# One group of transposes in place of three: own rows, sample rows and sample residual

## The reference

```python
q = (xf @ w_q).reshape(n, PEER_HEADS, 2, PEER_DK // 2)
s = jnp.einsum('nhpd,hpkd->nhpk', q, sub_keys)
sv, si = lax.top_k(s, PEER_TOPK)                # 16 of 128 keys, twice
...                                             # 16 of the 256 pairs: eidx (experts), g (gates)
act = gelu(jnp.einsum('nd,ned->ne', xt, u[it])) * gt
y = jnp.einsum('ne,ned->nd', act, v[it])
h = h + y
```

## Time and profile before

| | |
|---|---|
| median of the runs, us | 1998.24 (1996.53 to 1999.02) |
| the profiled execution, us | 1998.43 |
| its span in the trace, us | 1996.6 |
| share of busy time | PE 98%, DVE 77%, ACT 43%, POOL 35% |
| granted clock of TensorE | 0.997 of full speed |
| DMA, mean over the span | 266 GB/s |

### The profile page before, as it was taken

One profiled execution on the slowest core, in us unless ns is written; L12 is line 12 of the kernel. 1 busy time (PEld: TensorE's weight loads), 2 busy tenths in 40 slices (PEclk: granted clock), 3 DMA queues, 4 the chain that ended last, 5 costly groups with the idle time before them and its releaser, 6 DMA issues.

```text
span 1996.6 us, 29304 instructions
## 1 busy us (share of the span) xinstructions
PE 1960.7 (98%) x11128; PEld 1748.1 (88%) x11128; DVE 1532.0 (77%) x2295; ACT 856.1 (43%) x865; POOL 701.6 (35%) x496
## 2 busy tenths in 40 slices
PE   7999999999999999999999999999999999999998
PEld 6997777998999999999999999988888888888886
DVE  4998756556788899889888997567777767778776
ACT  4340135434535555545455545533343433334343
POOL 2010101220526687888876883010100101113410
PEclk9999999999999999999999999999999999999999
DMA  5463295443444788888888898899988899998984
GB/s 209 162 202 132 98 383 207 148 168 127 152 145 149 258 275 273 291 279 293 279 291 280 313 338 288 295 343 345 344 325 332 328 349 352 361 354 342 376 316 145
DMA packets 101227, 531.29 MB, mean 266 GB/s; under 512 B 19376, under 2 KB 21568, under 8 KB 45792
## 3 DMA queue, kind: packets, MB, share of 16 engines
q1 hardware_dynamic: 71552, 408.93, 57.1%
q0 software_dynamic: 24304, 106.45, 14.4%
q10 hardware_dynamic: 5296, 14.98, 2.0%
HBM read 491.34 MB, written 38.14 MB: 265 GB/s over the span
## 4 chain that ended last, share of the span: by engine, by line
PE 88%; DVE 6%; issue 2%; ACT 2%; DMA 1%; POOL 0%; DVEq 0%; SPq 0%; ACTq 0%; POOLq 0%
PE acc L1616 18%; PE mis L1994 17%; PE acc L1994 17%; PE acc L1617 9%; PE acc L1593 5%; PE acc L1595 5%; PE acc L1594 5%; PE acc L1642 5%; PE acc L1736 2%; DVE wl L932 2%; DMA raw<-in_u 1%; PE mis L1711 1%; ACT wh L545 1%; DVE xhl L940 0%; PE mis L1687 0%
## 5 line engine op out<-in xcount | busy, mean ns | idle before, releaser
L932 DVE TENSOR_TENSOR wl<-raw,wh 128x2048 fp32r<-128x2048 f32 x310 | 711.3, 2296 | 280.0 <-ACT wh L545 263.8
L545 ACT ACTIVATE wh<-raw 128x2048 fp32r<-128x2048 f32 x310 | 593.2, 1915 | 568.4 <-DMA raw<-in_v 403.7
L1616 PE MATMUL acc<-xhl,wh 128*128 128x448 f32 x2048 | 643.1, 374 | 1.0 <-DVE wl L932 1.0
L1617 PE MATMUL acc<-xhl,wl 128*128 128x224 f32 x2048 | 541.2, 264 | 0.0
L1616 PEld LDWEIGHTS acc<-xhl,wh 128*128 128x128 f32 x2048 | 384.1, 188 | 31.5 <-DVE wl L932 2.0
L1617 PEld LDWEIGHTS acc<-xhl,wl 128*128 128x128 f32 x2048 | 390.7, 191 | 0.0
L2152 POOL DMA_INDIRECT G<-gsum,cell x224 | 342.7, 1530 | 79.8 <-issue 68.2
L1593 PE MATMUL acc<-xhl,wh 128*128 128x288 f32 x736 | 220.7, 300 | 15.0 <-DVE wl L968 14.1
L1594 PE MATMUL acc<-xhl,wh 128*128 128x288 f32 x736 | 217.7, 296 | 0.0
L1595 PE MATMUL acc<-xhl,wl 128*128 128x288 f32 x736 | 217.4, 295 | 0.0
L2108 POOL DMA_INDIRECT ring<-in_ur,eidx x32 | 38.6, 1206 | 334.5 <-DVE hs L1421 325.9
(11 more groups left out here) (336 smaller groups left out, 2633.1 us busy)
## 6 DMA issues: line engine op xcount, KB each, us to landing
raw<-in_u SPq DMA_DIRECT2D x128, 1024.0 KB
raw<-in_v SPq DMA_DIRECT2D x128, 1024.0 KB
raw<-in_w_mix SPq DMA_DIRECT2D x28, 1024.0 KB
G<-zero SPq DMA_DIRECT2D x16, 1024.0 KB, 13.6
raw<-in_w_out SPq DMA_DIRECT2D x16, 1024.0 KB
raw<-in_w_pq SPq DMA_DIRECT2D x16, 1024.0 KB
gin<-G SPq DMA_DIRECT2D x32, 512.0 KB
h<-hbg ACTq DMA_DIRECT2D x32, 448.0 KB
```

What stands on the lines that cost most here:

```text
L545: act.activation(wh[:, n % 4], raw[:, n % 4], ACT.Copy).then_inc(hi_done, 1)
L932: dve.tensor_tensor(wl[:, n % 4], raw[:, n % 4], wh[:, n % 4].bitcast(F32), ALU.subtract).then_inc(lo_done, 1)
L1616: pe.matmul(acc[:, s, 0:2 * NU], wh[:, s, j, :], xu[:, j, 0:2 * NU], start=(j == 0), stop=False)
L1617: ins = pe.matmul(acc[:, s, 0:NU], wl[:, s, j, :], xuh[:, j, :], start=False, stop=(j == DT - 1))
```

## The change

The three groups become one, in step 2 of u. `xs4` is now filled with four different things: own columns (part 0 and 3), the sample's normed columns (part 1, by DVE, `sample_rows` moved from step 114 to step 0) and the sample's residual columns (part 2). One `turn_rows` makes rows of all three. ACT copies them out in steps 3 and 4, two banks each. In step 5 it writes partitions 32 to 63 to DRAM (`sample_rows`) and 64 to 95 (`hst_rows`), and in step 6, when both have landed, it copies the own rows from partitions 0 to 31 over these two parts, inside SBUF. The first own dot waits for that. In SP's program the sample rows are loaded back into the four parts of `xrow`, 256 KB each, one after each of the tiles 124 to 127. The first load has a wait for the last own dot ahead of it, behind a wait for the own tokens' hidden values that was there before. The sample's dots, Gelu and sums all stand two steps of v later. PE's groups 29 and 30 are back in the loop.

```diff
-V_DOTS = {2 * n: n for n in range(PICKS)}
-V_GELU = 2 * PICKS
+V_DOTS = {2 * n + 2: n for n in range(PICKS)}
+V_GELU = 2 * PICKS + 2
...
                     load_own_hidden(0)
+                    sp.wait_ge(dot_a_done, PICKS_A)
+                    sp.wait_ge(xr_out, 16)
+                if 124 <= n < 124 + P // NS:
+                    q = n - 124
+                    sp.dma_start(xrow[NS * q:NS * q + NS, :], dr["xr"]).then_inc(xrow_in, 16)
...
+            def row_copies():
+
+                act.wait_ge(xrow_out, 4)
+                act.dma_start(dr["xr"], xrow_a[NS:2 * NS, :]).then_inc(xr_out, 16)
+                act.dma_start(dr["hst"], xrow_a[2 * NS:3 * NS, :]).then_inc(hst_out, 16)
+
+            def row_repeats():
+
+                act.wait_ge(xr_out, 16)
+                act.wait_ge(hst_out, 16)
+                for q in (1, 2):
+                    act.dma_start(xrow_a[NS * q:NS * q + NS, :], xrow_a[0:NS, :]).then_inc(xrow_a_in, 16)
+
+            def rows_together():
+
+                act.wait_ge(xs_ready, 1)
+                for q in (0, 3):
+                    act.activation(xs4[:, :, q, :], xs[:], ACT.Copy).then_inc(xs4_ready, 1)
+                act.activation(xs4[:, :, 2, :], hT[:, :, NP_:N], ACT.Copy).then_inc(xs4_ready, 1)
...
-                if n == 4 * XROW_IT - 1:
-                    four_times(2)
-                if 3 <= n < 7:
-                    row_evac(xrow_a, n - 3, 1)
...
+                for c in ROW_EVACS.get(n, ()):
+                    row_evac(c)
+                if n == ROW_COPIES:
+                    row_copies()
+                if n == ROW_REPEATS:
+                    row_repeats()
...
-            with pe.Fori(1, XROW_IT) as i:
+            with pe.Fori(1, 31) as i:
                 for s in range(4):
                     u_slot(i, s)
             for s in range(4):
-                u_slot(XROW_IT, s)
-                if s == TURN_S:
-                    pe.wait_ge(xrow_out, 4)
-                    pe.wait_ge(xs4_ready, 2)
-                    turn_rows()
-            for s in range(4):
-                u_slot(HST_IT, s)
-                if s == TURN_S:
-                    pe.wait_ge(xrow_out, 8)
-                    for c in range(DT):
-                        ins = pe.transpose(mis[0:NS, c // 4, P * (c % 4):P * (c % 4) + P], hT[:, c, NP_:N], ident)
-                    ins.then_inc(hst_turned, 1)
-            for s in range(4):
                 u_slot(31, s)
```

More of the change, by code:

```diff
@@ L74 @@
 RSTD = (1, 0, 0, 1, 0)
-XROW_IT, HST_IT, TURN_S = 29, 30, 1
-XROW_EVAC, HST_EVAC = 4 * XROW_IT + TURN_S + 1, 4 * HST_IT + TURN_S + 1
+ROW_EVACS, ROW_COPIES, ROW_REPEATS = {3: (0, 1), 4: (2, 3)}, 5, 6
 CO_NEXT = {8: 2, 11: 3}
@@ L309, in build @@
                 xs4 = sb(o, "xs4", [P, DT, P // NS, NS])
-            with ExitStack() as o:
-                hst = sb(o, "hst", [P, D])
         ring_a = (ring_a0, ring_a1, ring_a2)
@@ L373, in build @@
         dot_done, sgelu_done, sact_ready, vsum_done = sem("dot_done"), sem("sgelu_done"), sem("sact_ready"), sem("vsum_done")
-        hst_turned, hst_copied, hst_out, hst_in = sem("hst_turned"), sem("hst_copied"), sem("hst_out"), sem("hst_in")
+        xrow_in, xrow_a_in, hst_out, hst_in = sem("xrow_in"), sem("xrow_a_in"), sem("hst_out"), sem("hst_in")
+        xr_out = sem("xr_out")
         res_turned, part_in, part_sum = sem("res_turned"), sem("part_in"), sem("part_sum")
@@ L824, in _, with row_evac @@
             act.sem_inc(gelu_done, 1)
-            def row_evac(to, c, count):
+            def row_evac(c):
                 if c == 0:
[L829 to L840, removed]
+                    act.wait_ge(xrow_turned, 1)
+                act.activation(xrow_a[:, 512 * c:512 * c + 512], mis[:, c, :], ACT.Copy).then_inc(xrow_out, 1)
+            def row_copies():
[12 more added lines that the diff above has]
+                act.activation(xs4[:, :, 2, :], hT[:, :, NP_:N], ACT.Copy).then_inc(xs4_ready, 1)
             def gelu_a(c):
@@ L858, in u_hook @@
                 if n == 1:
-                    four_times(1)
-                if n == 4 * XROW_IT - 1:
-                    four_times(2)
-                if 3 <= n < 7:
-                    row_evac(xrow_a, n - 3, 1)
[L864 to L871, removed]
+                    rows_together()
+                for c in ROW_EVACS.get(n, ()):
[4 more added lines that the diff above has]
+                    row_repeats()
                 if n == 4 * 31 + 2:
@@ L1401, in sample_rows @@
             def sample_rows():
-                dve.wait_ge(xrow_turned, 1)
-                own.done(dve.tensor_tensor(xs[:], hT[:, :, NP_:N], bcast(par[:, Q_GFFN:Q_GFFN + DT], NS, 2), ALU.mult))
+                dve.wait_ge(xs_ready, 1)
+                at = xs4[:, :, 1, :]
+                own.done(dve.tensor_tensor(at, hT[:, :, NP_:N], bcast(par[:, Q_GFFN:Q_GFFN + DT], NS, 2), ALU.mult))
                 own.wait(0)
-                dve.tensor_tensor(xs[:], xs[:], bcast(rstd[:, 1, NP_:N], DT, 1), ALU.mult).then_inc(xs_ready, 1)
+                dve.tensor_tensor(at, at, bcast(rstd[:, 1, NP_:N], DT, 1), ALU.mult).then_inc(xs4_ready, 1)
             def own_dot(g):
@@ L1411, in own_dot @@
                     dve.wait_ge(xrow_out, 4)
+                    dve.wait_ge(xrow_a_in, 32)
                 dve.wait_ge(pick_a_in[own_ring(g)], 16 * len(ring_users(g)))
@@ L1418, in pick_dot @@
                 if g == 0:
-                    dve.wait_ge(xrow_out, 8)
+                    dve.wait_ge(xrow_in, 16 * (P // NS))
                 dve.wait_ge(pick_in[g % 2], 16 * (g // 2 + 1))
@@ L1461, in u_extras @@
                     own_x()
+                    sample_rows()
                 if n == 4:
@@ L1938, in _ @@
                     pe.wait_ge(pq_out, 16)
-                    pe.wait_ge(xs4_ready, 1)
+                    pe.wait_ge(xs4_ready, 4)
                     turn_rows()
-            with pe.Fori(1, XROW_IT) as i:
+            with pe.Fori(1, 31) as i:
                 for s in range(4):
@@ L1944, in _ @@
             for s in range(4):
[L1945 to L1957 removed]
                 u_slot(31, s)
             def residual():
[L1962 removed]
+                pe.wait_ge(xrow_out, 4)
                 for t in (1, 0):
@@ L2277 @@
     dr["ha"] = nc.dram_tensor("h_own", (P, NKEYS, NA), F32, kind="Internal").ap()
+    dr["xr"] = nc.dram_tensor("sample_rows", (NS, D), F32, kind="Internal").ap()
     dr["hst"] = nc.dram_tensor("hst_rows", (NS, D), F32, kind="Internal").ap()
```

3 lines of the change are left out of this document (removed).

## The result

The kernel after the change took 2002.18 us (median of 11 runs, 1998.43 to 2007.87), the kernel before 1999.02 us beside it (11 runs). The ratio is 1.0019, with a 95% interval of 1.0011 to 1.0027, so the change costs some 3.8 us (the two medians alone differ by 3.2). I had forecast 1996.0 us. The 3.8 us are just inside the 4.0 us that I had called no change (0.85), but the sign is wrong, and the range (to 1999.3) does not hold the time. The time is that of the rival to which I gave 0.06 (2001.9 us). Only its number fits; how it got there is told under the rivals.

What follows compares the result with a forecast made beforehand. PE was taken to bound the kernel, at 88% of the chain. The terms -3.32, +0.8 and +0.3 summed to -2.2 us, from 1998.24 to 1996.0 us, with a stated range of 1994.1 to 1999.3.

Steps and rivals of the forecast that it cites:

- Removed from PE, -3.32: The second and third groups of transposes, at 1234 and 1256, leave PE's program: 1.66 us each, 3.32 us gained.
- DVE's and ACT's removed work, nothing: Operations leaving steps 114 and 115 and eight evacuations gain zero, since DVE and ACT were not waited for there.
- Steps 0 to 7 of u, +0.8: Steps 0 to 4 free; in 5 to 7 ACT's DMAs make tile 9 late, PE waits at tile 10: 0.8 us, bounds 0 and 3.2.
- Tiles 124 to 127, +0.3 with a bound of 1.3: End of u: PE comes earlier than the loads of tiles 124 and 125 allow: 0.3 us lost, bounds 0 and 1.3.
- half rate: Rival at tiles 124 to 127: 32-partition pieces take 1.4 us each, 0.2 to 0.7 us more, 1996.5 us; chance 0.10.
- Second product, nothing: In v, the sample's dots and sums two steps later cost nothing, with 6.6 us of margin at PE's tile 122.
- A small load holds SP's queue: Rival ahead of v: each `xrow` piece holds SP's queue 3.7 us, costing 6.2 us, 2001.9 us in all; chance 0.06.
- The full gain: Rival: no wait arises at tile 10 or tiles 124 and 125, so -3.3 us, 1994.9 us; chance 0.33.
- ACT's wait: Rival at u's start: slow landings of ACT's DMAs make tile 10 late by 3.2 us, 1998.4 us; chance 0.13.

Runs made afterwards that it cites:

- e1: The changed kernel without the four `xrow` loads, ACT filling `xrow` with other numbers in step 118: 1997.91 us, ratio 0.9992 to the kernel before.
- e8: The changed kernel with loads behind tiles 119 and 120, dots, Gelu and sums at their old steps, `al` ahead of DVE's last remainder tile: 1995.84 us, ratio 0.9984.
- e11: The changed kernel with loads behind tiles 119 and 120 and the dots, Gelu and sums at their old steps, `al` not moved: 1997.0 us, ratio 0.9988.
- e3: The changed kernel with the same four loads behind tiles 119 and 120, two each, dots still two steps later: 1998.03 us, ratio 0.9994.
- e2: The changed kernel with each load over 128 partitions by 512 columns, from sample rows written to DRAM four times (three more writes on ACT's queue): 2007.25 us, ratio 1.0041.
- e6: The kernel before plus only the four 32-partition loads behind tiles 124 to 127, reading rows of u: 2003.2 us, ratio 1.0019.
- e7: The changed kernel with only the first two loads, ACT filling the other half of `xrow` in step 118: 2000.21 us, ratio 1.0001.
- e5: The kernel before with only the sample's dots, Gelu and sums two steps of v later: 1999.48 us, ratio 1.0001.
- e10: The kernel before with only `al` moved ahead of the second v tile's remainder in DVE's last u step: 1999.05 us, ratio 0.9999.
- e9: The changed kernel with only `al` moved ahead of the second v tile's remainder in DVE's last u step: 2000.41 us, ratio 1.0006.

## Why the prediction was wrong, step by step

**Removed from PE, -3.32: right.** From tile 108 to tile 122 the traces after gain 3.4 (e1) to 3.7 us (after, e8, e11).

**DVE's and ACT's removed work, nothing: not contradicted.** e3 and e11, which lose nothing at the end of u, come out at 0.9994 and 0.9988. The intervals of both hold the 0.9987 (-2.5 us) that the first terms alone give. A cost of 1 to 2 us would stay hidden.

**Steps 0 to 7 of u, +0.8: right in sum, with luck.** The start took 52.9 to 53.5 us in the five traces with u's start unchanged (mean 53.1), and 53.3 to 55.0 in the eight with the change's (mean 54.0): 0.9 us more. The change's own trace shows 0.2. The parts were off in both directions, and the sum hides it. The two writes landed after 4.4 and 5.5 us in place of 4.2, but their issue took 0.35 and 0.44 us in place of 0.63; then tile 9 was held by its own load:

```profile
676.89 1.20 ACTq L846 DMA_DIRECT2D xrow_a<-xrow_a  x2
679.38 1.92 ACT L548 ACTIVATE wh<-raw 128x2048 fp32r<-128x2048 f32 x1 [2.78 <-DMA raw<-in_u]
```

It started 1.65 us later than in the earlier trace rows, with PE's tile 0 0.9 us later as well.

**Tiles 124 to 127, +0.3 with a bound of 1.3: this step failed.** It cost 7.7 us in the trace, and the loads alone 5.4 by the runs (e1). Three things in it were wrong.

- *The price of a piece.* I took 0.7 us, 256 KB at the 383 GB/s of the earlier trace rows. From 1261 to 1277 the change moved 279 GB/s at full engines, e2 407: 16 us x 279 / 407 = 11.0 us, so 5.0 us were lost over four pieces, 1.25 us each on top of 0.64, together 1.9 us. The same working gives less for e6: 16 us x 315 / 407 = 12.4 us, 0.9 us lost each, 1.5 us a piece. I call these estimates, since other loads share the stretch. I had even named the mechanism, as "half rate", at 1.4 us a piece, and gave it 0.10. By the Trainium skill, "SBUF — State Buffer", section "Door 1: The DMA port swizzle", 32 partitions reach half of the ports, 189 GB/s; the holes of 172 to 229 GB/s agree with that.
- *Which tiles pay.* I let only the pieces ahead of tile 125 count, because the share of 1265 to 1290 was 0.74, and so priced half rate at 0.2 to 0.7. But four pieces pushed a full queue 5 us back, through tiles 124 to 127 into both v tiles, before the quiet part could take it up. The kernel before, in stretches of 5 us, shows why the mean misled: 1.9 us were free from 1265 to 1270 (a share of 0.62), and next to nothing from 1270 to 1275.

```profile
1265.00:1270.00 5.00, 5.00 (x34) 4.77 (x33) 3.20 (x3) 4.56 (x5) 0.00 (x0) 1.00 0.62 205
1270.00:1275.00 5.00, 5.00 (x33) 4.78 (x32) 2.92 (x3) 3.29 (x3) 0.00 (x0) 1.00 0.98 329
```

- *The margin ahead of v.* I took 2.1 us, from the end of `al` to v. Behind `al` DVE has `hbg`, without which PE can't start the second half of the residual's transposes. Two rows of the kernel before (DVE, then PE) would have told me: `hbg` ended at 1289.76, and PE wanted it after eight of the sixteen transposes, half of the 1.67 us between 1289.39 and 1291.06, at 1290.2. That is 0.5 us. e1 confirms it: without any load, a PE 1.5 us early waited 1.25 us there.

```profile
1289.14 0.62 DVE L1325 TENSOR_TENSOR hbg<-acc,hsum 128x448 f32<-128x448 f32 x1
```

```profile
1289.39 1.91 PE L1967 MATMUL acc<-cst,hT 128*128 128x128 f32 x16
1291.06 1.17 PE L1994 MATMUL mis<-wh,ah 128*128 128x512 f32 x4
```

And a stop costs more than its length. Behind the 3.46 us the granted clock was 0.68 from 1295 to 1300, a mean between full speed (2.4 GHz) and the lower level (1.2 GHz). The eight transposes took 1.62 us (1294.89 to 1296.51) in place of half of 1.67 us for sixteen, and the first four multiplies of v 1.77 us in place of 1.01 us: 1.5 us together. The stops of 1.92 us in e7 and 3.09 us in e2 cost 1.7 and 1.6 us more in the same way. Behind e1's wait of 1.25 us the clock stayed at 1.00.

**Second product, nothing: right** (e5, 1.0001).

**The rivals.** "A small load holds SP's queue" gave the measured time by luck. It had the right place, pieces that hold up SP's queue into v, but a price of 3.7 us each, twice what was measured, against a margin of 2.1 us and 6.5 us of free time that were both too large; the errors cancel. With 1.9 us a piece its own sum (4 x 1.9 - 2.1 - 6.5) is below zero, so its "decides from about 1.7 us" was wrong as well. "Half rate" had the right mechanism, and fell short in the tiles that pay. The queue rival's argument against ("SP's loads pass at 383 GB/s with pieces of 128 to 512 KB among them") compared by bytes. Those pieces (`hin` and `gin`, split along their second dimension) all fill 128 partitions; the likeness to ask for was one in partitions. The full gain (1994.9) was nearly reached by e8, with other places for the loads and two more edits whose share isn't shown. ACT's wait was no part of it here; e2 shows that it could have been: five writes in place of two cost 3.7 us at the start (56.98 against 53.3).

My own range was put together wrongly too: -3.3 to +1.3 about the median with 1 us of scatter on both sides is 1993.9 to 2000.5, not 1994.2 to 1999.5. That doesn't hold the time either.

What stays open: how much of a narrow piece's cost is the shape and how much its source in DRAM, and why the change (14.5 us to land, 1.9 us a piece) was slower than e6 (11.4, 1.5) with loads of one shape. The small waits of PE between tiles 11 and 117 sum to 0.3 us in e10 and 2.5 in e6, both with u's tiles unchanged there; I take them for differences between executions.

## What to carry to other kernels

Price a transfer by the partitions that it fills, not only by its bytes: here 256 KB into 32 partitions held a full queue for an estimated 1.5 to 1.9 us, into 128 for 0.64. Put a transfer that nobody waits for soon where the queue has room now, not where the mean of the next 25 us says so. When a bound engine comes earlier, list every operation that it takes at the next stage, down to the last small one, and take the smallest margin: a gain ahead of a fixed arrival is only wait.

## What the runs showed of the hardware

- The share of busy DMA engines doesn't show a shape that moves slowly: 1.02 at 279 GB/s and 1.02 at 407 GB/s in the same 16 us. Only the GB/s beside it do.
- In a full queue, narrow pieces slow single packets: 225 of 536 packets of 8 KB took over 0.5 us in the change, against 10 of 497 in e2, where the median is 0.31. The busy share counts the slow packets as busy.
- Stops of PE of 1.25 (e1), 1.38 (e9) and 1.69 us (the change, tile 125) left the granted clock at 1.00; behind stops of 1.92 (e7), 2.34 (e6), 3.09 (e2) and 3.46 us (the change) it was 0.66 to 0.68 over the next 5 us.
- In the change's trace copies from SBUF to SBUF of 256 KB, issued by ACT, landed after 7.5 and 10.2 us, when the writes of the same size to DRAM took 4.4 and 5.5.
